# Threshold selection by tiles inside the attention's steps, rotations beside the last projections, and another order in layer 1's steps

## What is computed

```python
logits = jnp.einsum('bthd,bsd->bths', q_idx, k_idx) * IDX_DIM ** -0.5
score = jnp.einsum('bth,bths->bts', w_idx, jax.nn.relu(logits))
score = jnp.where(causal[None], score, -jnp.inf)
_, sel = lax.top_k(score, n_sel)            # mixer A attends to these keys
...
p = p[:, 0] - lam * p[:, 1]                 # layer 1
o = jnp.einsum('bgrts,bsge->btgre', p, v)
```

## Time and profile before

| | us |
|---|---|
| median of three runs | 2282.15 |
| profiled execution, device time | 2285.52 |
| its span, first to last instruction | 2283.7 |
| dense projections and MLP of layer 0 (669 to 1255) | 586 |
| layer 0's steps (322 to 669) | 347 |
| layer 1's steps and head norm (1411 to 1684) | 273 |

### The profile page before, as it was taken

How to read it: one execution, slowest core, us unless ns; L and a number is a source line. 1 busy time by engine, 2 the same in 40 slices (tenths; PEclk the granted TensorE clock), 3 DMA queues, 4 the chain that set the end, 5 groups by cost and what they waited for, 6 DMA issues and landing times.

```text
span 2283.7 us, 32506 instructions
## 1 busy us (share of the span) xinstructions
PE 2009.0 (88%) x11272; PEld 1443.8 (63%) x11272; DVE 742.9 (33%) x1642; ACT 420.9 (18%) x771; POOL 267.4 (12%) x482
## 2 busy tenths in 40 slices
PE   7889957887768999999998997777788999999996
PEld 5447624544556777777776772344466777777775
DVE  2268975646501421110001421655523311200002
ACT  1120114454502200000001200333333100000000
POOL 3000221221110000000000000232200000000000
PEclk9999977988779999999999998998899999999998
DMA  7101053967641122111211113888701221212111
GB/s 236 41 22 64 0 218 142 338 237 271 231 176 65 56 70 68 64 65 65 73 64 64 48 63 119 283 291 266 263 21 54 69 69 64 73 57 73 64 65 59
DMA packets 95091, 264.45 MB, mean 116 GB/s; under 512 B 13650, under 2 KB 20051, under 8 KB 94355
## 3 DMA queue, kind: packets, MB, share of 16 engines
q0 software_dynamic: 46560, 167.80, 20.9%
q1 hardware_dynamic: 44146, 88.86, 11.5%
q10 hardware_dynamic: 4288, 6.51, 0.8%
HBM read 255.30 MB, written 7.82 MB: 115 GB/s over the span
## 4 chain that ended last, share of the span: by engine, by line
PE 70%; DVE 16%; DVEq 3%; ACT 3%; issue 3%; ACTq 2%; DMA 2%; SPq 1%; PEldq 0%
PE ps L485 53%; DVE arena L1427 4%; PE ps L541 2%; PE ps L842 1%; DVE arena L1308 1%; DVE small L1684 1%; PE ps L907 1%; DMA arena<-in_kv_ab 1%; PE ps L730 1%; PE ps L862 1%; PE ps L706 1%; PE ps L666 1%; DVEq L1312 1%; ACT arena L1219 1%; ACTq L329 1%
## 5 line engine op out<-in xcount | busy, mean ns | idle before, releaser
L485 PE MATMUL ps<-hs,wring 128*128 128x288 f32 x3520 | 872.4, 411 | 24.9 <-ACT hs L993 16.4
L485 PEld LDWEIGHTS ps<-hs,wring 128*128 128x128 f32 x3520 | 675.0, 192 | 220.5 <-issue 20.1
L485 PE MATMUL ps<-arena,wring 128*128 128x288 f32 x2048 | 500.5, 408 | 5.7 <-DVE arena L1342 5.7
L485 PEld LDWEIGHTS ps<-arena,wring 128*128 128x128 f32 x2048 | 391.0, 191 | 115.3 <-issue 6.6
L414 POOL DMA_DIRECT2D wring<-in_weights x170 | 90.2, 530 | 1386.3 <-PE ps L485 1385.0
L1340 DVE TENSOR_TENSOR arena<-arena,norm 128x576 f32 x64 | 48.5, 758 | 371.6 <-ACT arena L1012 365.2
L1297 DVE TENSOR_TENSOR norm<-norm 128x576 f32<-128x576 f32 x24 | 18.2, 759 | 448.6 <-ACT norm L1003 448.6
L1012 ACT ACTIVATE arena<-ps 128x576 f32 (+1 forms) x76 | 49.5, 651 | 527.2 <-PE ps L485 527.2
L1003 ACT ACTIVATE norm<-ps 128x576 f32<-128x576 f32 x32 | 20.8, 651 | 631.7 <-PE ps L485 631.7
L344 POOL DMA_DIRECT2D arena<-in_kv_ab x128 | 68.7, 537 | 278.6 <-PE ps L716 155.7
L344 POOL DMA_DIRECT2D arena<-in_kv_c x128 | 68.7, 537 | 215.6 <-PE ps L907 95.6
(11 more groups left out here) (231 smaller groups left out, 1804.8 us busy)
## 6 DMA issues: line engine op xcount, KB each, us to landing
wring<-in_weights POOLq DMA_DIRECT2D x174, 512.0 KB, 3.7
arena<-in_kv_ab SPq DMA_DIRECT2D x128, 320.0 KB, 5.0
arena<-in_kv_ab POOLq DMA_DIRECT2D x128, 320.0 KB, 6.5
arena<-in_kv_c SPq DMA_DIRECT2D x128, 256.0 KB, 4.0
arena<-in_kv_c POOLq DMA_DIRECT2D x128, 256.0 KB, 4.6
arena<-in_w_v_ab SPq DMA_DIRECT2D x1, 2592.0 KB, 24.6
xs<-in_x_t SPq DMA_DIRECT2D x4, 576.0 KB, 9.3
out_y_t<-xs SPq DMA_DIRECT2D x4, 576.0 KB, 2.8
```

Source lines behind the costliest of these rows:

```text
L485: mm = pe.matmul(out[:, h * 512:h * 512 + TH], wring[:, slot, k], inp[:, b * KD + k, h * TH:(h + 1) * TH], start=(b == 0 and k == 0), stop ...
```

## The change

There are three parts. (1) After the search VectorE finishes only the samples' tile. The three prompt tiles are finished by a new function chosen(t) in steps 1 to 3 of layer 0's attention, after q_mix(t - 1) and ahead of q_max(t); tile 0 needs none. The small values of the search move to another place in the arena, which holds the indexer's key until it is stored, so the wait for that store (ik_stored) and a memset stand ahead of the search. (2) The five rotations follow the last five of the 13 projections, in the other pair of PSUM buffers, instead of the five value tiles; the loop over the projections is written out. TensorE waits for the last rotation's copy before the first value tile. The rotated chunks are waited for on VectorE after the selection. (3) In layer 1 the unit's turn comes first in a step, the samples' turns come up to a quarter earlier and ahead of the values that need them, the sums come at the end of step n for unit n - 2 instead of n - 3, and ScalarE's and VectorE's orders follow.

```diff
@@ -238,6 +237,7 @@
         UNITS_A, UNITS_AB, STEPS_AB = 16, 32, 40
+        ROT_A = 8
@@ -313,7 +313,9 @@
         assert SEL_AT[4] <= 4 * T
-        selw = area(tr0 + 2 * SEL_AT[4], 64)
+        selw = area(KPAD + 640, 64)
+        eq_p, cum_p, out_p = (area(512 * j, 512) for j in range(3))
+        assert KPAD + 704 <= N_I * T
         cnt, sgn, kk, thr_b, keep_f, above, rest = (selw[:, 4 * j:4 * j + 4] for j in range(7))
@@ -615,25 +615,26 @@
             pe.wait_ge(PH["I"]["read"], len(UNITS_OF["I"]) * BODIES["I"])
-            dense(G_AB + N_I, O_AB + N_I, N_AB - N_I, hs, peel=1)
-
-            def rotate_a(j):
-
-                if j == 0:
-                    pe.wait_ge(dense_out, N_AB)
-                if j >= 2:
-                    pe.wait_ge(rope_read, j - 1)
+            def rotate_a(j, jstat, static):
+
+                c = j - ROT_A
+                if c < 0:
+                    return
+                pe.wait_ge(dense_out, N_I + c + 1)
+                if c >= 2:
+                    pe.wait_ge(rope_read, c - 1)
                 for h in range(2):
-                    mm = pe.matmul(ps[j % 2][:, h * 512:h * 512 + TH], C["rot"], qk[:, AQ + j, h * TH:(h + 1) * TH],
+                    mm = pe.matmul(ps[2 + c % 2][:, h * 512:h * 512 + TH], C["rot"], qk[:, AQ + c, h * TH:(h + 1) * TH],
                                    start=True, stop=True)
...
-            token_major(0, wv, 640, 16, after=rotate_a)
+            dense(G_AB + N_I, O_AB + N_I, N_AB - N_I, hs, peel=N_AB - N_I, after=rotate_a)
+            pe.wait_ge(rope_read, 5)
+            token_major(0, wv, 640, 16)
             pe.wait_ge(vtok_out, 5)
...
                 pe.sem_inc(kv_free[slot], 4)
-            pe.wait_ge(rope_read, 5)
-
+            pe.wait_ge(dense_out, N_AB)
             pe.wait_ge(rope_done, 10)
@@ -917,33 +918,35 @@
                 b, quarter = n // 4, n % 4
+                if 2 <= n < UNITS_C + 2:
+                    p_turn(n - 2)
                 if n < UNITS_C:
...
                     c_keys(b, 1)
+                if quarter == 0 and b:
+                    c_turn(b - 1, 0)
                 if quarter == 1 and b >= 2:
                     c_pick(b - 2)
+                if quarter == 1 and b:
+                    c_turn(b - 1, 1)
                 if quarter == 1 and b < NB:
...
                 if quarter == 1 and b:
-                    c_turn(b - 1, 0)
+                    c_turn(b - 1, 2)
                 if quarter == 2 and b:
-                    c_turn(b - 1, 1)
+                    c_turn(b - 1, 3)
                     c_values(b - 1, 0)
-                    c_turn(b - 1, 2)
                     c_values(b - 1, 1)
                 if quarter == 3 and b:
-                    c_turn(b - 1, 3)
+                    c_turn(b - 1, 4)
                     c_values(b - 1, 2)
-                    c_turn(b - 1, 4)
                     c_values(b - 1, 3)
...
                 if 2 <= n < UNITS_C + 2:
-                    p_turn(n - 2)
-                if 3 <= n < UNITS_C + 3:
-                    p_sums(n - 3)
+                    p_sums(n - 2)
             c_pick(NB - 1)
@@ -1068,14 +1071,16 @@
                 act.activation(two(qk[:, j]), halves(ps[(O_AB + j) % 2]), ACT.Copy, scale=SCALE if query else 1.0).then_inc(dense_out, 1)
+                c = j - N_I - ROT_A
+                if c >= 0:
+                    act.wait_ge(rot_done, N_I + c + 1)
+                    if c >= 2:
+                        act.wait_ge(rope_done, N_I + c - 1)
+                    act.activation(two(sqs[:, c % 2]), halves(ps[2 + c % 2]), ACT.Copy).then_inc(rope_read, 1)
             for t in range(5):
...
                 act.activation(vt[0:m, t, 0:640], ps[2 + t % 2][0:m, 0:640], ACT.Copy).then_inc(vtok_out, 1)
-                act.wait_ge(rot_done, N_I + t + 1)
-                if t >= 2:
-                    act.wait_ge(rope_done, N_I + t - 1)
-                act.activation(two(sqs[:, t % 2]), halves(ps[t % 2]), ACT.Copy).then_inc(rope_read, 1)
@@ -1245,23 +1250,21 @@
                 b, quarter = n // 4, n % 4
+                if 2 <= n < UNITS_C + 2:
+                    p_turn_out(n - 2)
                 if quarter == 0 and b < NB:
...
                     c_keys_out(b, 0)
-                if quarter == 1 and b < NB:
-                    c_keys_out(b, 2)
                 if n < UNITS_C:
...
                 if quarter == 1 and b < NB:
-                    c_keys_out(b, 3)
-                    c_keys_out(b, 4)
+                    for g in range(2, 5):
+                        c_keys_out(b, g)
                 if quarter == 3 and b < NB:
                     c_exp(b)
-                if 2 <= n < UNITS_C + 2:
-                    p_turn_out(n - 2)
             act.wait_ge(SM["c"]["done"], 8)
@@ -1420,9 +1423,9 @@
-            def count(src, scalar, op, out=junk):
-
-                for j in range(4):
+            def count(src, scalar, op, out=junk, tiles=4):
+
+                for j in range(tiles):
                     x = scalar if isinstance(scalar, float) else scalar[:, j:j + 1]
@@ -1440,6 +1443,8 @@
+            dve.wait_ge(ik_stored, 16)
+            dve.memset(qz0, 0.0)
             dve.drain()
@@ -1464,35 +1469,44 @@
-            count(scores, thr_b, ALU.is_gt)
+            count(scores, thr_b, ALU.is_gt, tiles=1)
             dve.tensor_tensor(cnt[:, 0:1], cnt[:, 0:1], other, ALU.add)
             dve.drain()
-            dve.tensor_tensor(rest, C["topk"], cnt, ALU.subtract)
-            dve.drain()
-            count(scores, thr_b, ALU.is_equal, out=flip)
+            dve.tensor_tensor(rest[:, 0:1], C["topk"][:, 0:1], cnt[:, 0:1], ALU.subtract)
+            dve.drain()
+            count(scores, thr_b, ALU.is_equal, out=flip, tiles=1)
...
             dve.drain()
-            for j in range(4):
-                dve.tensor_tensor_scan(cum[j], flip[j], flip[j], init_s if j == 0 else 0.0, ALU.add, ALU.bypass)
-            dve.drain()
-            for j in range(4):
-                dve.scalar_tensor_tensor(flip[j], cum[j], rest[:, j:j + 1], flip[j], ALU.is_le, ALU.mult)
-            dve.drain()
-            for j in range(4):
-                dve.scalar_tensor_tensor(flip[j], scores[j], thr_b[:, j:j + 1], flip[j], ALU.is_gt, ALU.add)
-            dve.drain()
-            for j in range(4):
-                dve.tensor_scalar(scores[j], flip[j], -1.0, BIG, ALU.add, ALU.mult)
-            dve.drain()
-
-            dve.sem_inc(sel_done, 1)
-            dve.wait_ge(rope_done, 10)
-            dve.wait_ge(ik_stored, 16)
-            dve.memset(qz0, 0.0)
+            dve.tensor_tensor_scan(cum[0], flip[0], flip[0], init_s, ALU.add, ALU.bypass)
+            dve.drain()
+            dve.scalar_tensor_tensor(flip[0], cum[0], rest[:, 0:1], flip[0], ALU.is_le, ALU.mult)
+            dve.drain()
+            dve.scalar_tensor_tensor(flip[0], scores[0], thr_b[:, 0:1], flip[0], ALU.is_gt, ALU.add)
+            dve.drain()
+            dve.tensor_scalar(pen_s, flip[0], -1.0, BIG, ALU.add, ALU.mult)
             dve.memset(s_a[:, KN:KPAD], 0.0)
...
             dve.drain()
+            dve.wait_ge(rope_done, 10)
+
+            def chosen(j):
+
+                w = SEL_W[j]
+                thr = thr_b[:, j:j + 1]
+                dve.tensor_scalar(out_p[:, 0:w], scores[j], thr, None, ALU.is_gt, ALU.add, accum_out=cnt[:, j:j + 1])
+                dve.tensor_scalar(eq_p[:, 0:w], scores[j], thr, None, ALU.is_equal, ALU.add, accum_out=cnt[:, 0:1])
+                dve.drain()
+                dve.tensor_tensor(rest[:, j:j + 1], C["topk"][:, j:j + 1], cnt[:, j:j + 1], ALU.subtract)
+                dve.tensor_tensor_scan(cum_p[:, 0:w], eq_p[:, 0:w], eq_p[:, 0:w], 0.0, ALU.add, ALU.bypass)
+                dve.drain()
+                dve.scalar_tensor_tensor(eq_p[:, 0:w], cum_p[:, 0:w], rest[:, j:j + 1], eq_p[:, 0:w], ALU.is_le, ALU.mult)
+                dve.drain()
+                dve.tensor_tensor(eq_p[:, 0:w], eq_p[:, 0:w], out_p[:, 0:w], ALU.add)
+                dve.drain()
+                dve.tensor_scalar(scores[j], eq_p[:, 0:w], -1.0, BIG, ALU.add, ALU.mult)
+                dve.drain()
+
             ph, sm = PH["AB"], SM["ab"]
@@ -1624,6 +1638,8 @@
                     q_mix(t - 1)
+                if 1 <= t < 4:
+                    chosen(t)
                 if t < UNITS_A:
@@ -1748,8 +1764,14 @@
                 b, quarter = n // 4, n % 4
+                if 3 <= n < UNITS_C + 3:
+                    p_out(n - 3)
                 if n < UNITS_C:
                     p_max(n)
+                if quarter == 1 and b >= 2:
+                    c_out(b - 2)
+                if quarter and b:
+                    c_turn_out(b - 1, (1, 3, 4)[quarter - 1])
                 if 1 <= n < UNITS_C + 1:
@@ -1757,27 +1779,19 @@
                         c_stage(b + 1)
+                    if b:
+                        c_turn_out(b - 1, 0)
                 if quarter == 1:
-                    if b >= 2:
-                        c_out(b - 2)
```

(19 more changed lines are left out.)

## The result

The kernel after takes 2225.1 us (median of four runs, 2222.1 to 2233.3), the kernel before 2281.9 (four runs, 2279.0 to 2286.1). The ratio is 0.9755, with a 95% interval of 0.9725 to 0.9786: faster by 57 us. The forecast was 2236 and its range 2217 to 2261. The profiled execution took 2233.3 us (span 2231.5), the slowest of the four; against that of before (span 2283.7) it is 52.2 shorter, where the sum had said 46. Runs of one kernel lie some 10 us apart, so whole times are compared by medians and places by traces.

What follows compares the result with a forecast made beforehand. Layer 0's selection end and layer 1's handoffs, with no engine full, were taken to hold TensorE: 2285.5 - 7.7 (layer 0) - 38 (layer 1) = 2239.8, on the median's scale 2236 us; range 2217 to 2261.

Steps and rivals of the forecast that it cites:

- C: Layer 1 rival: the reorder only renames the waits, layer 1 gains nothing, layer 0 its 7.7 us: 2274 us; chance 0.08.
- D: Layer 1 rival: the turn at the head blocks TensorE's step behind it, a batch takes 34.8 us: 2311 us; chance 0.05.
- B: Layer 1 rival: a new wait, late slots or p_mix at the head, replaces the old; period 27.5, 2257 us; chance 0.22.
- rival A: Layer 1: engines alone bound, TensorE's 21.6 us the limit, transfers keep up; period near 22.3, 2219 us; chance 0.17.
- Layer 1's period: Layer 1's steps: a batch falls from 29.5 to 24.5 us, between the two transfer bounds and nearer to the share.
- the seventh and the tail: Layer 1's end: the seventh period gains 5.0 us, the sample's turns and copies after the last exp 3, bounds 0 to 4.
- the extrapolation of the share: Layer 1's transfers: if their busy time stays what it is, a batch needs 0.85 x 29.5 = 25.1 us.
- the burst at 378 GB/s: Layer 1's transfers: 8.39 MB a batch, at the rate where both queues ran, take 22.2 us.
- TensorE's bound: Layer 1's steps: TensorE's busy share of the old step, 142.6 / 195 x 29.5, gives 21.6 us a batch.
- The first keys: Layer 0: the prompt tiles leave the selection's end, so TensorE's first sample keys come 9.7 us earlier, bounds 7 to 11.
- The fifth rotation: Layer 0's search: one more GpSimd rotation meets VectorE's rounds, costing 1.1 us, or up to three instructions, 4.2.
- Layer 0 in all: Layer 0: 9.7 us earlier less 2 exposed by the prompt tiles gives 7.7 us gained, bounds -2 and +10.

Runs made afterwards that it cites:

- turns_only: Kernel after with layer 1's unit turn and sums put back at the step's end, samples' turns kept early: 2256.7 us, ratio 0.9891.
- no_chosen: Kernel after without the three chosen(t) calls, so prompt tiles keep raw scores as their mask: 2225.4 us, ratio 0.9762.
- half_new: Kernel after loading only the left half of each layer 1 cache page, as many transfers at half the bytes: 2212.6 us, ratio 0.9698.
- part 3 alone: Kernel before with only layer 1's new step orders in the three engines' programs: 2236.1 us, ratio 0.9804.
- late_stores0: Kernel after with layer 0's four stores issued in step 6 instead of ahead of the steps: 2230.6 us, ratio 0.9769.
- Part 1 alone: Kernel before with only the selection by tiles, rotations and layer 1 as before: 2280.7 us, ratio 1.0.
- part 2 alone: Kernel before with only the rotations moved beside the last projections, selection and layer 1 as before: 2283.5 us, ratio 1.0005.
- half_old2: Kernel before loading only the left half of each layer 1 cache page, a repeat of a first such run: 2279.9 us, ratio 0.9988.
- late_stores: Kernel after with layer 0's four stores in step 6 and layer 1's three stores behind its steps: 2231.8 us, ratio 0.9777.

## Why the prediction was right

- **Where the gain lies.** Right: layer 1's chain of handoffs and the end of the selection. The exp's wait for the turn is gone from first place, TensorE is at 85% (123.91 of 145), the transfers' share is near 1. Rivals C and D are out; a period like B's 27.5 is what half of the reorder gives (`turns_only`: 26.7).
- **The time.** The range of 2217 to 2261 held, and the mechanism with it: handoffs went, transfers took over. The value was 11 us too high, and the period of 23.05 lies just outside the forecast's own 23.3 to 26.2, on the side of rival A.
- **Layer 1's period: 24.5 predicted, 23.05 measured** (22.2 to 23.6 in the traces with the same steps)**.** This is the term that was mis-sized. Six periods gave 38.5 us and not 30; the seventh and the tail gave 7.7 (from the last like score to the weighing), where I had 5.0 + 3. The step that failed is the extrapolation of the share: 0.85 x 29.5 = 25.1 took the busy time for each byte as fixed. It is not: 289 GB/s at 0.85 are 340 at full share, and 358 were moved at 0.99. Transfers that queue up are moved in less busy time each. The other end, 22.2 by the burst at 378 GB/s, was the nearer one (0.9 off, against 2.1). By the Trainium skill (DMA: Bandwidth & Descriptors, "Specifications"), which gives some 358 GB/s from HBM for a core, a batch takes 23.4 us as an estimate, 0.4 over the measured one. It is not a limit, though: `no_chosen` moved 373 GB/s over 135 us of layer 1's steps, and layer 0's loads ran at 396 GB/s for 16 us, as the hardware section shows.
- **TensorE's bound: 21.6 predicted, 20.2 measured** by `half_new` (19.4 of it busy). I had taken its busy time from a stretch with the granted clock at 0.94; in `half_new` it is 1.00, all the time at the 2.4 GHz level. Rival A's limit was thus too high, and A itself failed on the transfers, not on TensorE.
- **The first keys: 9.7 us earlier predicted, 9.3 to 9.5 measured.** The fifth rotation did not cost three instructions, and the store (ik_stored) that I had costed at 0 to 2.5 us costs nothing: no VectorE wait for it shows ahead of the search.
- **Layer 0 in all: 7.7 predicted, 4.0 at the absolute value, 5.5 at the end of the steps** (3.7 against the trace of part 3 alone)**.** Chosen costs 2.4 (predicted 2), so that step held. What failed is that the second group's key loads would be in by 321: one landed at 325.2. The slots came 2.0 us later than with part 3 alone and 3.6 than before, about the 2 predicted, but SyncE's first eight issues took 11.69 us and not the 6.30 of before, for which the prediction has no term. Late loads are not the whole of it: of the 5.3 us lost between first keys and absolute value `no_chosen` gives back 2.4 and `late_stores0`, with its quick issues, 0.6. The rest is not assigned by any run.
- **The 11 us between 2236 and 2225.** Layer 1 gained 8.8 more than the sum, layer 0 some 2 less: 6.5 by the profiled executions. The other 5 are the scale: this profiled execution lies 8.2 over its median, where I had taken off the 3.4 of before. Those 5 us are neither merit nor fault of the sum: another execution might have been profiled.

## What to carry to other kernels

When no engine is full, look in an engine's hand-written order for the instruction that the next step's head waits for and that stands at the end of this step; move it to the head, and issue what needs another engine's copy a step early. Before such a move, work out the period of each resource and expect the transfers to take over: half the bytes in as many transfers is a cheap test that tells whether they have. Two moves that each bring nothing alone may be worth making together, when each covers the other's wait; here that is shown at one place of layer 0 and not for the whole kernel. And before a few microseconds of one trace are given to a cause, look at other kernels' traces of the same code: here they lay up to 5 us apart in layer 1.

## What the runs showed of the hardware

**SyncE's issues slow down beside ScalarE's stores and GpSimd's loads.** Its first eight loads of keys took 6.3 us in the kernels in which GpSimd's loads come ten us later and ScalarE's stores five, 11.5 to 11.7 when both come at once, and 6.5 when GpSimd's come at once but the stores do not. So the stores are needed for it; whether the stores alone would do it no run shows. Part 1 alone, then part 2 alone, then the kernel after with the stores moved:

```profile
302.86 6.29 SPq L345 DMA_DIRECT2D arena<-in_kv_ab  x8
```

```profile
302.34 11.59 SPq L345 DMA_DIRECT2D arena<-in_kv_ab  x8
```

```profile
302.59 6.49 SPq L346 DMA_DIRECT2D arena<-in_kv_ab  x8
```

**Loads alone went at 396 GB/s for 16 us.** The kernel after, transfers by queue in layer 0's steps (332 to 348 us), where no store is left, and then the total in layer 1's steps (1460 to 1580 us):

```profile
DMA packets 2130, 6.34 MB, mean 396 GB/s; under 512 B 290, under 2 KB 290, under 8 KB 2129
...
arena<-in_kv_ab SPq DMA_DIRECT2D x8, 320.0 KB, 5.9
```

```profile
DMA packets 18439, 43.43 MB, mean 362 GB/s; under 512 B 2635, under 2 KB 2635, under 8 KB 18425
...
arena<-in_kv_c SPq DMA_DIRECT2D x84, 256.0 KB, 5.0
```

The busy share is near 1 in both. Halved rows of layer 1 gave a share of 0.65 at 202 GB/s, so the share isn't proportional to the bytes. Why pages of 256 KB go slower than pages of 320 KB (362 GB/s here, 373 in `no_chosen`) was not tried; in layer 1 some slots also come free late (GpSimd's wait for line 883).

**TensorE at a third of its rate with a granted clock of 1.00.** The first execution of the halved loads in the kernel before took 7109 us; another of the same kernel took 2277. Its span was 7107.5 us with a granted clock of 1.00. First the kernel before, then that execution, groups of the projections:

```profile
L485 PE MATMUL ps<-hs,wring 128*128 128x288 f32 x3520 | 872.4, 411 | 24.9 <-ACT hs L993 16.4 <-DVE hs L1287 3.2 <-DVE hs L1785 2.7
```

```profile
L486 PE MATMUL ps<-hs,wring 128*128 128x288 f32 x3520 | 3257.6, 1202 | 21.9 <-ACT hs L994 14.7 <-DVE hs L1786 2.7 <-DVE hs L1288 2.6
```

A matmul takes 1202 ns instead of 411, 2.9 times as long (not some four, as the expectation of `half_old2` has it). One execution of `late_stores` was as long (7091.6 us), also with a granted clock of 1.00. What slows TensorE there the records don't show.
